# A two-block transformer forward pass on one core: moving the mLSTM gate columns to another chunk of the input product, and reordering the first mixer

## The reference

```python
def mlstm_mixer(x, w_in, b_ig, b_fg, head_g, w_out):
    proj = x @ w_in                          # 256 x 3080: q 512, k 512, v 1024, o 1024, ig 4, fg 4
    q, k, v, o, ig, fg = jnp.split(proj, M_SPLITS, axis=-1)
    log_i = soft_cap(ig + b_ig)              # 15 * tanh(g / 15)
    log_f = jax.nn.log_sigmoid(soft_cap(fg + b_fg))
    h = mlstm_chunkwise(q, k, v, log_i, log_f)   # 4 heads; decays from cumulative sums of log_f
    h = layer_norm_per_head(h) * head_g
    return (jax.nn.sigmoid(o) * h) @ w_out
```

## Time and profile before

| quantity | value |
|---|---|
| median of three runs | 1161.36 us |
| the profiled execution, its device time | 1161.42 us |
| its span, first to last instruction | 1159.7 us |
| PE busy | 1151.3 us (99%) |
| DVE busy | 801.6 us (69%) |
| ACT busy | 623.8 us (54%) |
| DMA moved | 210.82 MB, mean 182 GB/s |
| share of the chain that ended last | PE 95% |

### The profile page before, as it was taken

How to read it: one execution, slowest core, us unless ns; L and a number is a source line. 1 busy time by engine, 2 the same in 40 slices (tenths; PEclk the granted TensorE clock), 3 DMA queues, 4 the chain that set the end, 5 groups by cost and what they waited for, 6 DMA issues and landing times.

```text
span 1159.7 us, 16804 instructions
## 1 busy us (share of the span) xinstructions
PE 1151.3 (99%) x6609; PEld 965.8 (83%) x6609; DVE 801.6 (69%) x1161; ACT 623.8 (54%) x954; POOL 39.5 (3%) x64
## 2 busy tenths in 40 slices
PE   9999999999999999999999999999999999999998
PEld 9888888888886788888888888888777788888887
DVE  6679655657888875565687666568778676566666
ACT  5465544444558544444556455447576775445555
POOL 2000000000000000000000000000102000000000
PEclk9999999999999999999999999999999999999999
DMA  8656565565654356546556555654553265655540
GB/s 290 210 208 219 176 205 182 185 206 190 200 190 143 122 201 201 199 164 214 186 167 195 182 187 176 217 181 135 202 183 110 85 198 184 216 183 188 176 179 37
DMA packets 119966, 210.82 MB, mean 182 GB/s; under 512 B 8320, under 2 KB 67024, under 8 KB 119888
## 3 DMA queue, kind: packets, MB, share of 16 engines
q1 hardware_dynamic: 119344, 209.35, 53.9%
q10 hardware_dynamic: 544, 0.40, 0.1%
HBM read 208.68 MB, written 1.05 MB: 181 GB/s over the span
## 4 chain that ended last, share of the span: by engine, by line
PE 95%; DVE 2%; ACT 1%; DMA 1%; issue 0%; POOL 0%; SPq 0%; ACTq 0%; DVEq 0%; POOLq 0%
PE psum L356 14%; PE psum L357 14%; PE psum L358 14%; PE psum L447 13%; PE psum L422 9%; PE psum L450 7%; PE psum L425 5%; PE psum L364 4%; PE psum L365 4%; PE psum L370 4%; PE psum L1667 1%; PE psum L1006 1%; PE psum L1705 1%; PE psum L1726 1%; DMA ring<-in_w_in 1%; DVE w_both L339 0%
## 5 line engine op out<-in xcount | busy, mean ns | idle before, releaser
L308 DVE TENSOR_TENSOR w_both<-ring,w_both 128x2048 fp32r<-128x2048 f32 x129 | 295.1, 2289 | 206.5 <-ACT w_both L299 206.4
L299 ACT ACTIVATE w_both<-ring 128x2048 fp32r<-128x2048 f32 x129 | 246.8, 1916 | 184.7 <-PE psum L358 134.8
L356 PE MATMUL psum<-w_both,hidT_high 128*128 128x512 f32 x432 | 168.6, 390 | 0.0
L358 PE MATMUL psum<-w_both,hidT_low 128*128 128x512 f32 x436 | 168.6, 387 | 0.0
L357 PE MATMUL psum<-w_both,hidT_high 128*128 128x512 f32 x432 | 168.5, 390 | 0.0
L447 PE MATMUL psum<-xT,w_both 128*128 128x512 f32 x640 | 159.9, 392 | 0.0
L447 PEld LDWEIGHTS psum<-xT,w_both 128*128 128x128 f32 x640 | 116.4, 189 | 21.7
L339 DVE TENSOR_TENSOR w_both<-ring,w_both 128x1024 fp32r<-128x1024 f32 (+4 forms) x97 | 115.1, 1213 | 7.4 <-ACT w_both L329 6.8
L329 ACT ACTIVATE w_both<-ring 128x1024 fp32r<-128x1024 f32 (+4 forms) x97 | 98.4, 1056 | 34.0 <-PE psum L358 18.8
L422 PE MATMUL psum<-xT,w_both 128*128 128x512 f32 x448 | 112.0, 392 | 0.0
L356 PE MATMUL psum<-w_both,xT 128*128 128x512 f32 (+4 forms) x256 | 97.9, 383 | 0.0
(11 more groups left out here) (381 smaller groups left out, 1651.1 us busy)
## 6 DMA issues: line engine op xcount, KB each, us to landing
ring<-in_mlp_w_up SPq DMA_DIRECT2D x32, 1024.0 KB, 5.5
ring<-in_mlp_w_down SPq DMA_DIRECT2D x32, 1024.0 KB, 5.0
ring<-in_ffn_wg SPq DMA_DIRECT2D x44, 512.0 KB, 4.0
ring<-in_ffn_wu SPq DMA_DIRECT2D x44, 512.0 KB, 5.0
ring<-in_ffn_wd SPq DMA_DIRECT2D x22, 1024.0 KB, 5.0
ring<-in_ple_w_gate SPq DMA_DIRECT2D x12, 1024.0 KB, 5.0
ring<-in_w_in SPq DMA_DIRECT2D x10, 1024.0 KB, 5.2
ring<-in_a_w_in SPq DMA_DIRECT2D x8, 1024.0 KB, 10.4
```

The source lines that it names most:

```text
L299: K.nc.scalar.activation(parts_of(K, n)[0][:, 0:w], K.ring[:, n % SLOTS, 0:w], ACT.Copy).then_inc(K.high_ready, 2)
L308: K.nc.vector.tensor_tensor(low[:, 0:w], K.ring[:, n % SLOTS, 0:w], high[:, 0:w].bitcast(F32), ALU.subtract).then_inc(K.low_ready, 2)
L356: nc.tensor.matmul(out, x[0], w[0], start=start, stop=False)
L358: return nc.tensor.matmul(out, x[1], w[0], start=False, stop=stop)
```

## The change

The 8 gate columns leave chunk 0 (now 384 columns) and go to the front of chunk 2 (now 392). Each DMA of loads 0 and 1 is then a single piece of 384 columns, while loads 4 and 5 come in three pieces (8, 128 and 256 columns), which were one piece of 384. The threshold in `half_of` goes from "up to 1536 elements" to "below 1536", so loads of 1536 elements are now split in two halves too (loads 0 and 1), and loads 4 and 5 (1568 elements) also come in halves. `gturn` waits for the third `take` instead of the first. The step lists of the three engines are written in another order, and so is DVE's list behind the mixer (`after_mlstm_dve`).

```diff
-    for spans in ([g(0, 1), q(0, 3)], [q(3, 4), k(0, 3)], [k(3, 4), v(0, 1)], [v(1, 3)], [v(3, 4), o(0, 1)], [o(1, 3)],
+    for spans in ([q(0, 3)], [q(3, 4), k(0, 3)], [g(0, 1), k(3, 4), v(0, 1)], [v(1, 3)], [v(3, 4), o(0, 1)], [o(1, 3)],
                   [o(3, 4)]):
...
-    if w <= SLOT * 3 // 4:
+    if w < SLOT * 3 // 4:
         return (0, w) if j == 1 else None
...
-    return {0: [(o[:, D:D + 8], 0, 8), (qk[:, 0:384], 8, 392)],
+    return {0: [(qk[:, 0:384], 0, 384)],
...
-            2: [(qk[:, 896:1024], 0, 128), (v[:, 0, :], 128, 384)],
+            2: [(o[:, D:D + 8], 0, 8), (qk[:, 896:1024], 8, 136), (v[:, 0, :], 136, 392)],
...
             elif step == "gturn":
-                pe.wait_ge(K.act_took.sem, 1)
-                pe.wait_ge(K.dve_took.sem, 1)
+                pe.wait_ge(K.act_took.sem, 3)
+                pe.wait_ge(K.dve_took.sem, 3)
...
-    return (392, 512, 384, 512, 512, 512, 256)[c]
+    return (384, 512, 392, 512, 512, 512, 256)[c]
```

More of the change, by code:

```diff
@@ L1081, in after_mlstm_dve @@
     yield "lead_low", 0, 0
+    yield "update", 0, 0
     yield "lead_low", 0, 1
-    yield "update", 0, 0
     yield "stats", 0, 0
@@ L1087, in after_mlstm_dve @@
     yield "spread", 0
+    yield "centre", 0, 1
     yield "centre", 0, 0
-    yield "centre", 0, 1
     yield "normal", 0, 0
@@ L1095, in after_mlstm_dve @@
     yield "stats", 1, 0
+    yield "update", 1, 1
     yield "low", 0, 0
-    yield "update", 1, 1
+    yield "low", 0, 1
     yield "stats", 1, 1
-    yield "low", 0, 1
     yield "spread", 1
+    yield "centre", 1, 1
     yield "centre", 1, 0
-    yield "centre", 1, 1
     yield "normal", 1, 0
@@ L3532, in pe_steps @@
         yield "xturn", 3
+        yield "dense", 0, 0, 0, range(2, 4)
         yield "dense", 0, 0, 1, range(2)
         yield "dense", 0, 0, 1, range(2, 4)
-        yield "dense", 0, 0, 0, range(2, 4)
         yield "dense", 0, 1, 0, range(4)
@@ L3538, in pe_steps @@
         yield "dense", 1, 0, 0, range(4)
-        yield "dense", 1, 0, 1, range(4)
-        yield "tiles", 0
-        yield "gturn",
         yield "dense", 1, 1, 0, range(4)
         yield "dense", 2, 0, 0, range(4)
+        yield "dense", 1, 0, 1, range(4)
         yield "dense", 1, 1, 1, range(4)
-        yield "colturn",
         yield "dense", 2, 0, 1, range(4)
         yield "dense", 2, 1, 1, range(4)
-        yield "gcol",
         yield "dense", 2, 1, 0, range(4)
+        yield "tiles", 0
         yield "dense", 3, 0, 0, range(4)
-        yield "scores", 0
+        yield "colturn",
+        yield "gturn",
+        yield "dense", 3, 0, 1, range(4)
         yield "tiles", 1
         yield "dense", 3, 1, 0, range(4)
+        yield "dense", 3, 1, 1, range(4)
+        yield "gcol",
+        yield "dense", 4, 0, 0, range(4)
+        yield "scores", 0
+        yield "dense", 4, 0, 1, range(4)
         yield "scores", 1
-        yield "dense", 3, 0, 1, range(4)
-        yield "dense", 3, 1, 1, range(4)
         yield "values", 0
         yield "scores", 2
-        yield "dense", 4, 0, 0, range(4)
         yield "values", 1
-        yield "dense", 4, 0, 1, range(4)
+        yield "scores", 3
         yield "values", 2
-        yield "scores", 3
+        yield "dense", 4, 1, 1, range(4)
         yield "dense", 4, 1, 0, range(4)
-        yield "dense", 4, 1, 1, range(4)
         yield "dense", 5, 0, 0, range(4)
@@ L3570, in pe_steps @@
         yield "dense", 5, 1, 1, range(4)
+        yield "dense", 6, 0, 1, range(4)
         yield "dense", 6, 0, 0, range(4)
-        yield "dense", 6, 0, 1, range(4)
         yield "zturn", 0, 0
@@ L3599, in act_steps @@
         yield "high", 2, 0
-        yield "take", 0, 0
         yield "high", 2, 1
@@ L3603, in act_steps @@
         yield "high", 3, 1
+        yield "high", 4, 0
         yield "high", 4, 1
-        yield "gturn",
+        yield "take", 0, 0
+        yield "high", 5, 0
         yield "high", 5, 1
@@ L3609, in act_steps @@
         yield "take", 1, 0
-        yield "colturn",
+        yield "take", 2, 0
         yield "tiles", 0
         yield "high", 7, 0
-        yield "gcol",
-        yield "take", 2, 0
         yield "high", 7, 1
         yield "high", 8, 0
+        yield "gturn",
         yield "high", 8, 1
+        yield "colturn",
+        yield "take", 3, 0
+        yield "high", 9, 0
+        yield "high", 9, 1
+        yield "gcol",
         yield "scores", 0
         yield "scores", 1
+        yield "values", 0
         yield "scores", 2
-        yield "take", 3, 0
-        yield "values", 0
-        yield "sin",
+        yield "high", 10, 0
         yield "values", 1
-        yield "high", 9, 0
-        yield "high", 9, 1
-        yield "high", 10, 0
+        yield "scores", 3
+        yield "values", 2
         yield "high", 10, 1
-        yield "values", 2
         yield "high", 11, 0
-        yield "scores", 3
+        yield "high", 11, 1
         yield "take", 4, 0
         yield "take", 4, 1
-        yield "high", 11, 1
         yield "high", 12, 1
         yield "values", 3
+        yield "sin",
         yield "high", 13, 1
         yield "take", 5, 0
+        yield "take", 5, 1
         yield "high", 14, 0
-        yield "take", 5, 1
         yield "high", 14, 1
@@ L3670, in dve_steps @@
         yield "low", 3, 1
+        yield "low", 4, 0
         yield "low", 4, 1
         yield "bias",
-        yield "gscan",
+        yield "angle",
+        yield "low", 5, 0
         yield "low", 5, 1
-        yield "gcol",
+        yield "take", 1, 1
+        yield "take", 2, 1
         yield "low", 6, 0
@@ L3678, in dve_steps @@
         yield "low", 7, 0
-        yield "take", 1, 1
-        yield "take", 2, 1
         yield "low", 7, 1
         yield "low", 8, 0
+        yield "tiles", 1
+        yield "gscan",
+        yield "low", 8, 1
+        yield "gcol",
+        yield "low", 9, 0
         yield "scores", 0
-        yield "angle",
+        yield "take", 3, 1
         yield "scores", 1
-        yield "tiles", 1
-        yield "low", 8, 1
+        yield "stats", 0
         yield "scores", 2
-        yield "take", 3, 1
-        yield "stats", 0
         yield "stats", 1
-        yield "low", 9, 0
         yield "low", 9, 1
@@ L3698, in dve_steps @@
         yield "scores", 3
+        yield "low", 11, 1
         yield "take", 4, 1
-        yield "low", 11, 1
         yield "low", 12, 1
```

## The result

| | before | after |
|---|---|---|
| median, 7 runs each | 1161.45 us | 1164.50 us |
| lowest to highest | 1161.36 to 1161.75 | 1164.31 to 1165.78 |
| ratio after / before | | 1.0028 [1.0018, 1.0037] |
| profiled execution, device time / span | 1161.42 / 1159.7 | 1165.78 / 1164.0 |

That is slower by 0.26% between the medians (by 0.18% at the least, by the interval of the ratio), and outside the range of 1160.5 to 1164.0. The execution that was profiled is the slowest of its seven. Two others of the same kernel were profiled later (experiments 8 and 12), and the differences between the three are part of the answer.

A forecast was written before the change was run, and what follows sets the result against it. PE, busy 99% of the span, was taken to bound the kernel. From the profiled 1161.42 us, +0.15 (start) +0.68 (heads) +0.3 (`values 3`) -0.1 (gate chain) -0.2 (switches) gave +0.8: 1162.2 us, "the same", range 1160.5 to 1164.0.

The forecast's parts named there:

- The start: PE's first transposes: x lands 0.3 us later, the second half's 0.16 us wait goes; +0.15 us, ends -0.7 and +0.5.
- rival (b): Start: a longer wait for x keeps PE at the lower clock for 12 matmuls of load 0; +2.1 us, 1164.3 us, 5%.
- The heads: Without `dense` cover, PE waits 0.27 us for DVE's product at `scores 2` and `scores 3`; +0.68 us in all, bounds +0.2, +1.5.
- `values 2`: Among the heads: waits for ACT's copy of head 1, now behind half of load 10; 0.14 us more.
- fewer switches: PE's list: two fewer changes between `dense` and other steps, 0.1 us each; -0.2 us.
- `values 3`: Late mixer step: waits for `take 4` of both tiles with only one `dense` as cover; +0.3 us, bounds 0 and 0.7.
- Loads 4 and 5: Weight loads, load 4 wanted 4 us sooner: both still ready in time; nothing, load 4's bounds 0 and +1.5 us.
- rival (a): The landing of load 4 or 5 decides: load 4 lands near 24 us, PE stalls 2.6 us; 1164.8 us, 10%.
- The gate chain: `gturn` near 41 us to `gcol` near 50: in time, old wait before `gcol` goes; -0.1 us, bounds -0.1 and +1.
- Chunks 0 and 2, and the rest: Eight columns move between matmuls of these chunks, one's loss the other's gain: 0; behind `values 3` nothing changes.
- Rival (c): The start wins: x lands early, both waits (0.84 us) go, heads' stalls stay at 0.2; 1160.5 us, 20%.

The follow-up runs named there:

- experiment 8: The changed kernel run again word for word, for its spread and a second profile: 1164.20 us, ratio 1.0023.
- 12: The changed kernel run once more word for word, for a third profile: the profiled execution took 1164.32 us.
- experiment 1: The kernel before, with ACT's two pieces of load 0 in the other order (384-column piece first): 1162.26 us, ratio 1.0011.
- 2: The changed kernel, with load 0 issued wholly by SP behind the first half of x and ACT's part removed: 1162.05 us, ratio 1.0006.
- 6: The kernel before, with both parts of load 0 issued by SP behind the first half of x: 1161.81 us, ratio 1.0003.
- experiment 4: The changed kernel, with two `dense` steps of chunk 4 between the heads again and the splits of ACT and DVE following: 1168.68 us, ratio 1.0061.
- experiment 9: The changed kernel, with `dense` steps between the heads again and `take 4` of both tiles ahead of `scores 3` on ACT and DVE: 1163.75 us, ratio 1.0019.
- 7 ones: The changed kernel, with 7 instead of 4 matmuls of ones on PE ahead of the transposes, profiled three times: 1164.23 us, ratio 1.0022.
- experiment 5: The changed kernel with the edits of 2 and experiment 9 together: 1161.37 us, ratio 0.9999.
- experiment 7: The changed kernel's orders on all engines, with the chunks, DMA pieces and `half_of` threshold of the kernel before: 1162.71 us, ratio 1.0011.

## Why the prediction was wrong

**The start (+0.15 us, ends -0.7 and +0.5): about +2.3. This step failed**, in two parts.

*The size of x's delay.* I put 0.5 us as the upper end: half of the 384 KB ahead of x's last bytes, at 388 GB/s. x came 1.9 us later. Both factors were wrong. The queue of ACT had moved 0.37 MB of its 0.39 by 6.4 us, when x was 0.4 us from landing: nearly all of the piece lay ahead of x's last bytes, not half. Before, it had moved 0.08 MB at that point. And 388 GB/s is the rate of 9 to 13.5 us; in these first microseconds it was 262 in the earlier trace rows. I had blamed the small pieces for that low rate. After has none in these loads, and moves no more (3 to 6 us, and the next 1 us):

```profile
3.00:6.00 3.00, 2.02 (x5) 1.02 (x4) 1.00 (x17) 0.00 (x0) 2.81 (x11) 1.00 0.90 237
6.00:7.00 1.00, 0.15 (x1) 0.16 (x2) 0.00 (x0) 0.00 (x0) 0.09 (x1) 1.00 1.06 399
```

384 KB (0.393 MB) at 237 GB/s are 1.7 us, near the 1.9 measured. Experiments 1, 2 and 6 fix the cause: x lands after 5.6 to 6.1 us in each of the kernels whose ACT queue has the big piece at its head, and after 3.8 to 4.1 us in each of the others.

The Trainium skill (DMA: Bandwidth & Descriptors, "Queues, rings and completion order") was cited for the sign, that an engine alternates between queues a packet at a time. The runs agree with the sign. By that rule the shorter of two transfers issued together would be through while the longer still runs, so that all of it lies ahead, which is the estimate of 1.7 us. The trace agrees nearly: ACT's piece landed 0.3 us behind x (6.3 and 6.0 us), so a little of it did not. I had the rule and did not carry it through.

*What the delay brings with it.* I priced rival (b), half of the start at the lower clock, at 2.1 us and gave it 5%, because "nothing shows that 0.3 us of idling does this". It was 2.5 us of idling: all three profiles of after, and those of experiments 4 and 9 with the same gap, run at half pace for a time behind x, and none of the three with 7 ones does. Of the start's loss some 1.2 us is lateness (the profiles with 7 ones), and in after's three profiles 0.9 to 2.3 us is the clock. So the right answer was the forecast's mechanism (x late) at six times the size put for it (1.9 us for 0.3), with rival (b) on top.

That the idling causes the half pace is not shown. Half pace behind the first transpose also occurs with next to no idling: in before until about 7.2 us (0.68 us of idling) and in experiment 5 until about 7.3 (0.41 us). It does not occur in experiments 2, 6 and 7 (0.34 to 0.60 us), nor in experiment 1 (2.11 us). And 7 ones also keep PE at work for longer. What the profiles do show is that it was cheap where x was early: experiment 7, at full pace from 4.90 on, has chunk 1 only 0.14 us ahead of before, since at full pace PE waits for load 0 and the second half of x instead (0.6, 0.3 and 0.3 us). Where x is late, that slack is gone, and in the five profiles with 2.4 us of idling or more half pace ends only at 9.5 to 12.9 us. What decides its length from one execution to the next was not settled, and no run of the lower clusters of after or of the higher one of experiment 1 was profiled. Nor are more ones a remedy that the median would show: it is 0.2 us below that of after's 18 runs, and level with that of experiment 8.

**The heads (+0.68, ends +0.2 and +1.5): right.** Each of the two waits costs about 0.25 us between starts (63.02 instead of 62.79, 65.74 instead of 65.46; 0.27 was forecast, from 54.65, the start of the last matmul of `scores 2`, and not from 54.67, which is the next `dense`), `values 2` nothing visible; the whole middle is +0.73, and experiment 9 gives 0.58 of it back. The 0.2 us that fewer switches between `dense` and other steps were to give cannot be seen: the heads and `gcol` leave some 0.1 us of the middle unexplained, in the other direction.

**`values 3` (+0.3, ends 0 and 0.7): 0.** PE's last `dense` was cover enough. Experiment 4 shows that the risk was real and which order brings it.

**Loads 4 and 5, rival (a) (10%): did not happen.** No wait for line 339; ACT waits for PE. After's x, and with it PE, came late, which gave the loads still more room, but experiment 5, with the early start, has no such stall over 0.2 us either. The piece with 32-byte runs did no harm there.

**The gate chain (0, -0.1): right in time, wrong in wait.** `gturn` at 44.27 and `gcol` at 53.48 us lie at the forecast's 41 and 50 plus the late start of 3.4; the wait before `gcol` stayed (0.4 us on the list of waits, 0.09 us between PE's starts).

**Chunks 0 and 2, and the rest (0): right.** The last stretch is the same to 0.04 us. Rival (c), a start that wins, had the sign of x's landing wrong: the small pieces were not what slowed x, but what kept the big one away from it.

## What to carry to other kernels

While the first load that everything waits for is in flight, put nothing large at the head of another queue, and price what does lie there in full, at the rate of that stretch and not of a later one. When a change makes TensorE idle for microseconds, allow for a lower clock behind the gap (0 to 2.3 us in the profiles here), and compare several profiles, for this part varies. When the cover between two dependent steps goes, the loss is the chain less the cover that is left, which rows give to a tenth of a microsecond; but look at once at what the moved cover had protected where it stood.

## What was not expected of the hardware

- The DMA engines moved 232 to 303 GB/s from 3 to 5.5 us in the fourteen profiles, whatever the pieces and queues, at a busy share of 0.89 or more, and 333 to 413 GB/s from 6 to 7 us. Why is open.
- An idle stretch of TensorE of 2.6 to 2.8 us was followed by 3.4 us at a granted clock of 0.50 in two places (experiment 8, 8.2 to 11.6 us; experiment 4, 78.0 to 81.4 us), in both 0.7 us or more after it had taken up work again at full pace.
- Near the start the column of granted clock read 1.00 where the lengths of equal instructions show half pace (after, 8.2 to 11.6 us), and read 0.50 for the same lengths in another execution.
